# Decoder layer with 32 experts on one core: part of the first expert's weights loaded before the expert loop, routing and last layer norm in another order

## The reference, cut to what matters

```python
logits = xf @ w_router + b_router
top_logit, top_idx = lax.top_k(logits, 4)
gates = jax.nn.softmax(top_logit, axis=-1)
# for each expert e, on the rows that chose it
gu = xblk @ w_gate_up[e] + b_gate_up[e]          # 1024 -> 2048
g, u = jnp.split(gu, 2, axis=-1)
act = (jnp.clip(u, -7, 7) + 1.0) * jnp.minimum(g, 7) * jax.nn.sigmoid(1.702 * jnp.minimum(g, 7))
y_rows = act @ w_down[e] + b_down[e]             # 1024 -> 1024
# gated sum over the four experts of a row, then
x = layer_norm(ALPHA * x + y, ln3_g, ln3_b)
```

## Time and profile before

| what | value |
|---|---|
| median of three runs | 1255.53 us |
| profiled execution, its time | 1254.92 us |
| profiled execution, span of the profile | 1253.1 us |
| PE busy | 1193.6 us (95%) |
| DMA over the span | 485.46 MB, mean 387 GB/s |
| expert weights among it | 403 MB |
| granted TensorE clock, mean | 0.997 of full speed |

### The profile page before, as it was taken

One profiled execution on the slowest core, in us unless ns is written; L12 is line 12 of the kernel. 1 busy time (PEld: TensorE's weight loads), 2 busy tenths in 40 slices (PEclk: granted clock), 3 DMA queues, 4 the chain that ended last, 5 costly groups with the idle time before them and its releaser, 6 DMA issues.

```text
span 1253.1 us, 16715 instructions
## 1 busy us (share of the span) xinstructions
PE 1193.6 (95%) x6623; PEld 564.9 (45%) x6623; DVE 364.7 (29%) x909; ACT 233.5 (19%) x444; POOL 46.1 (4%) x84
## 2 busy tenths in 40 slices
PE   9999999999999999999989999898989899989997
PEld 8994477877343433434332333233333333333333
DVE  4747734635222130211212030302021221212132
ACT  4543312223220201102020201010110102020101
POOL 2201000101100000000000000000000000000001
PEclk9999999999999999999999999999999999999998
DMA  9995997989799999999999999999999999999994
GB/s 324 255 319 187 294 304 271 377 343 420 266 423 423 428 428 428 425 428 427 430 426 427 427 427 427 427 427 424 428 429 427 426 427 426 431 424 427 426 425 189
DMA packets 65349, 485.46 MB, mean 387 GB/s; under 512 B 6664, under 2 KB 7052, under 8 KB 37056
## 3 DMA queue, kind: packets, MB, share of 16 engines
q1 hardware_dynamic: 60896, 469.35, 92.6%
q0 software_dynamic: 4224, 15.48, 3.8%
q10 hardware_dynamic: 192, 0.11, 0.0%
HBM read 479.75 MB, written 5.17 MB: 387 GB/s over the span
## 4 chain that ended last, share of the span: by engine, by line
PE 63%; DMA 33%; DVE 2%; ACT 1%; SPq 1%; issue 1%; POOL 0%; DVEq 0%; POOLq 0%
PE ps L2255 27%; DMA late<-in_w_gate_up_dram 16%; DMA ring<-in_w_gate_up_dram 14%; PE ps L1781 11%; PE ps L2313 6%; PE ps L2295 5%; PE ps L1828 5%; DMA late<-in_w_down_dram 3%; PE ps L2219 1%; PE ps L1970 1%; PE ps L2321 1%; PE ps L1992 1%; PE ps L2141 1%; PE ps L2164 1%; PE ps L2280 0%
## 5 line engine op out<-in xcount | busy, mean ns | idle before, releaser
L2255 PE MATMUL ps<-ring,arena 128*64 128x512 f32 x1536 | 360.1, 600 | 13.5 <-DMA ring<-in_w_gate_up_dram 13.5
L1678 DVE TENSOR_TENSOR arena<-arena,ps 128x264 f32<-128x264 f32 x128 | 55.1, 431 | 576.3 <-PE ps L2313 576.3
L2255 PEld LDWEIGHTS ps<-ring,arena 128*64 128x64 f32 x1536 | 99.8, 136 | 198.6 <-issue 164.1
L2295 PE MATMUL ps<-ring,arena 128*64 128x512 f32 x768 | 171.9, 596 | 14.7 <-DMA ring<-in_w_down_dram 14.4
L1088 ACT ACTIVATE arena<-arena 128x512 f32<-128x512 f32 x32 | 20.2, 632 | 470.6 <-DVE arena L1661 470.6
L2295 PEld LDWEIGHTS ps<-ring,arena 128*64 128x64 f32 x768 | 53.8, 137 | 119.1 <-issue 105.2
L2313 PE MATMUL ps<-arena 128*128 128x264 f32 x256 | 91.3, 438 | 0.0
L2255 PE MATMUL ps<-late,arena 128*64 128x512 f32 x384 | 90.2, 598 | 0.0
L1781 PE MATMUL ps<-arena,ring 128*128 128x256 f32 x384 | 88.1, 380 | 0.0
L2313 PEld LDWEIGHTS ps<-arena 128*128 128x128 f32 x256 | 38.1, 188 | 103.8 <-issue 103.8
L1781 PEld LDWEIGHTS ps<-arena,ring 128*128 128x128 f32 x384 | 70.8, 189 | 10.9 <-issue 1.8
(11 more groups left out here) (329 smaller groups left out, 953.5 us busy)
## 6 DMA issues: line engine op xcount, KB each, us to landing
ring<-in_w_gate_up_dram SPq DMA_DIRECT2D x96, 2048.0 KB, 33.8
ring<-in_w_down_dram SPq DMA_DIRECT2D x40, 2048.0 KB, 34.4
late<-in_w_gate_up_dram SPq DMA_DIRECT2D x16, 2048.0 KB, 33.9
arena<-in_w_gate_up_dram SPq DMA_DIRECT2D x16, 1024.0 KB, 32.2
late<-in_w_gate_up_dram SPq DMA_DIRECT2D x16, 1024.0 KB, 34.1
late<-in_w_down_dram SPq DMA_DIRECT2D x8, 2048.0 KB, 35.3
ring<-in_w_in_dram SPq DMA_DIRECT2D x11, 1024.0 KB, 19.9
ring<-in_cache_mem_k_dram SPq DMA_DIRECT2D x8, 1024.0 KB, 6.5
```

Source lines behind the costliest of these rows:

```text
L1678: nc.vector.tensor_tensor(xT[:, c, :], xT[:, c, :], ps[:, 2 + c % 2, 0:T], ALU.add).then_inc(e_y_out, 1)
L2255: ins = mm(ps[64 * j:64 * j + 64, 6 * a + gu, :], x, w[:, D * gu + 512 * j:D * gu + 512 * j + 512], start=(c < 0), stop=(c == 7), skip_gro ...
L2295: ins = mm(ps[64 * j:64 * j + 64, 4 + half, :], x, w[:, kk, 512 * half:512 * half + 512], start=(m == 0), stop=(m == 7), skip_group_check= ...
```

## The change

1. SP gets two loads before the loop's own: 1 MB of `w_down` of expert 0 (its item 16, the first of unit 8) into `ahead`, which is the place of `xh2` and later `g3`, and 512 KB (half of item 17) into `ahead_third`, the place of `yo`. They wait for what POOL's gain loads waited for. The load of unit 8 is then 512 KB. The first `down` reads the three places.
2. POOL's 11 gain loads wait for `e_du` 1, the first down item read by PE, since `ahead` lies where `g3` goes.
3. DVE's `low_of(1)` comes after `select(0)`, and PE's `gather` takes the samples and tile 0 first and tile 1 after them, with a wait for `s_least` 2 between.
4. PE's first pair and second pair are written out before the loop, and the two register loads that the loop's bounds need come after them.
5. The tail takes the sample rows first on PE and DVE, and ACT issues three of the four sample stores, SP one.
6. Two single 128x128 products (`stay_awake`) are added on PE in the second layer norm.

```diff
+        ahead = view(m0 + 4864, 2, D)
+        ahead_third = view(a_tail, D)
...
+            sp.wait_ge(s_rt, 1)
+            sp.wait_ge(s_hi, 2)
+            sp.wait_ge(s_less, 2)
+            sp.dma_start(ahead.rearrange("p v n -> p (v n)"), first_down[:, 0, :]).then_inc(landed_part[0], 16)
+            sp.dma_start(ahead_third, first_down[:, 1, 0:D]).then_inc(landed_part[1], 16)
             for u in range(UNITS, ROUND // 2):
                 unit_read(0, u - UNITS)
-                unit_load(0, u)
+                if u == UNITS:
+                    sp.dma_start(expert_slot(2 * u + 1)[:, D:2 * D], first_down[:, 1, D:2 * D]).then_inc(
+                        unit_landed(u), 16)
+                else:
+                    unit_load(0, u)
...
-            pool.wait_ge(s_hi, 2)
-            pool.wait_ge(s_less, 2)
-            pool.wait_ge(s_rt, 1)
+            pool.wait_ge(e_du, 1)
             pool.dma_start(g3[:, 0, :], ln3_g.broadcast_to((P, D))).then_inc(s_g3, 16)
...
-                for b in range(2):
+                for b in range(3):
                     act.dma_start(y_sample.rearrange("b s d -> (b s) d")[:, 256 * b:256 * b + 256],
...
-            low_of(1)
             dve.wait_ge(s_rt_out, 1)
...
             select(0)
+            low_of(1)
...
+                if k == 1:
+                    stay_awake(1, ps[:, 5, 0:P])
                 pe.wait_ge(s_dn_out, 40 if k == 0 else 56)
...
+                    for t in range(2):
+                        for c in range(4 * half, 4 * half + 4):
...
+                            elif between and half == 0 and c == 0:
+                                pe.wait_ge(s_least, 2)
...
-            pairs = pe.value_load(nswi[0:1, 0:1], min_val=16, max_val=80)
-            last_round = pe.value_load(nswi[0:1, 2:3], min_val=7, max_val=39)
...
-            with pe.Fori(0, last_round) as r:
+            pair(0, 0, first=True)
+            pair(0, 1)
+            pairs = pe.value_load(nswi[0:1, 0:1], min_val=16, max_val=80)
+            last_round = pe.value_load(nswi[0:1, 2:3], min_val=7, max_val=39)
+            with pe.Fori(1, last_round) as r:
...
+            for half, h in ((0, 0), (1, 0), (0, 1), (1, 1)):
+                copied(half, h)
+                b = 2 * half + h
+                ins = mm(ps[32 * b:32 * b + 32, LASTB[2], 0:256], SelT[:, half, SROWS:SROWS + 32],
+                         yb[:, half, 256 * h:256 * h + 256], start=False, stop=True, skip_group_check=True)
+                if b == 0:
+                    last_scatter(LORDER[0], 0, 0)
             ins.then_inc(s_ln, 1)
```

More of the change, by code:

```diff
@@ L336, in decoder_layer @@
         g3s = view(a_bgu + D + D // 2, 2, 256)
+        ahead = view(m0 + 4864, 2, D)
+        ahead_third = view(a_tail, D)
         landed = [sem(f"landed{s}") for s in range(RING)]
         landed_extra = [sem(f"landed_extra{i}") for i in range(2)]
-        landed_end = [sem(f"landed_end{i}") for i in range(2)]
+        landed_part = [sem(f"landed_part{i}") for i in range(2)]
         s_const = sem("s_const")
@@ L732, in _ @@
             sp.wait_ge(s_yo, 2)
-            for b in range(2, 4):
-                sp.dma_start(y_sample.rearrange("b s d -> (b s) d")[:, 256 * b:256 * b + 256],
-                             yo[32 * b + 32 - NS:32 * b + 32, 2, 0:256]).then_inc(s_yst, 16)
+            sp.dma_start(y_sample.rearrange("b s d -> (b s) d")[:, 3 * 256:4 * 256],
+                         yo[P - NS:P, 2, 0:256]).then_inc(s_yst, 16)
             sp.wait_ge(s_yst, 16 * 6)
@@ L2069, in layer_norm @@
                         sample_rows()
+                if k == 1:
+                    stay_awake(1, ps[:, 1, 0:P])
                 for c in range(4, DC):
@@ L2281, in turn_act, with down @@
                 ins.then_inc(e_at, 1)
-            def down(r, k, behind=None):
+            def down(r, k, behind=None, first=False):
                 for i in range(4):
-                    item_arrived(pe, r, ITEM_AT[k, 8 + i])
                     w = expert_slot(ITEM_AT[k, 8 + i]).rearrange("p (k n) -> p k n", k=2)
+                    if first and i == 0:
+                        pe.wait_ge(landed_part[0], 16)
+                        w = ahead
+                    else:
+                        item_arrived(pe, r, ITEM_AT[k, 8 + i])
+                    w = [w[:, v, :] for v in range(2)]
+                    if first and i == 1:
+                        pe.wait_ge(landed_part[1], 16)
+                        w[0] = ahead_third
                     for kk in range(2):
@@ L2343, in samples_turned, with pair @@
                 mm(ps[:, LASTB[2], 256:512], ident, g3s[:, 1, :], start=False, stop=True, skip_group_check=True)
-            def pair(r, j, last=False):
+            def pair(r, j, last=False, first=False):
                 it = 2 * r + j
@@ L2356, in pair @@
                 pe.wait_ge(e_at_out, 2 * it + 2)
-                down(r, 2 * j, sum_first if last else None)
+                down(r, 2 * j, sum_first if last else None, first)
                 pe.wait_ge(e_act, 2 * it + 3)
```

81 lines of the change are left out of this document (42 added, 39 removed).

## The result

The changed kernel takes 1262.76 us (median of 5 runs, 1261.8 to 1264.75) where the kernel before takes 1255.53 (5 runs, 1254.86 to 1257.22): 1.0058 times, with a 95% interval of 1.0047 to 1.0068. That is slower, as forecast, but by 7.2 us and not by the forecast's 2.5 (1258.0 against 1255.53), and outside the range. The profiled execution after has 1262.76 us and a span of 1260.95, against 1254.92 and 1253.11: the spans differ by 7.8 us, and this is the number that the traces have to explain.

The account below looks back on a forecast made before the run. It took the continuous DMA weight stream at 427 GB/s, then 28 us of tail, as the bound. Terms -1.2 + 3.9 + 0 + 0 + 0.1 = +2.8 us on 1254.92 gave 1257.7, raised to 1258.0 toward the median; range 1254.6 to 1260.4.

Parts of the forecast that it names:

- 1.5 MB ahead: Weight loads from unit 8 on: loading 1.5 MB early shortens the stream, -1.2 us taken, bounds 0 to -2.2.
- gain loads in the plateau: POOL's gain loads, moved to about 359 us into the full DMA stream, cost +3.9 us.
- first expert's start: Selection, gather and loop entry on PE: first expert begins about 320.75 us, no change; bounds -0.5 to +0.7.
- tail: Kernel's end with sample rows first and stores split three to one: +0.1 us, bounds -0.5 to +0.6.
- between the unit that the row shows and the best case: Loads of units 9 to 13: -1.2 us, chosen between unit 9's 0.5 us gain and 2.2 us at best.
- 3.2 us of idle DMA: Between the rest of unit 8 and unit 9: 3.2 of the 3.7 us saved become a DMA gap.
- Both bounds, 3.2 and 4.55 us: Price of POOL's late gain loads: 3.2 us by bytes at 427 GB/s, 4.55 by engine time held; middle taken.
- rival that they run beside the stream: Late gain loads at 359 to 366 us: a second queue lifts the rate to some 600 GB/s, costing nothing; 12%.
- lower sum, -2.7: Whole kernel, gain loads free, loads ahead at their best, half of the start's 0.5 gained: -2.7 us, 1252.2.
- The register loads go behind the second pair: nothing: PE near 425 us: register loads placed there cost nothing, since PE runs ahead of the DMA.
- DVE starts about when it did: Tail: sample products, 0.64 us, precede the first tile's second scatter half, so DVE's start hardly moves.
- The first tile's scale comes some 0.5 us later: Tail on DVE: sample statistics come first, delaying the first tile's scale some 0.5 us, carried through POOL's passes to its store.

Follow-up runs that it names:

- not_ahead: The changed kernel with the 1 MB and 512 KB loads issued by SP in unit 8's old place instead of ahead: 1262.67 us, 1.0069.
- no_tail: The changed kernel with the old tail put back: 1262.46 us, 1.0056 times the kernel before.
- gains_late: The kernel before with only POOL's 11 gain loads made to wait for the first down item, nothing loaded ahead: 1259.74 us, 1.0034.
- selection_only: The kernel before with the remainder behind the selection, the new gather order and the two idle products: 1256.33 us, 1.0008.
- pairs_out: The kernel before with PE's first two pairs written out ahead of the loop and the register loads behind them: 1256.55 us, 1.0012.
- third_ahead: The changed kernel with the old tail, gain loads at their old time and only 512 KB loaded ahead: 1257.08 us, 1.0014.
- gains_by_sp: The kernel before with the gain loads late, issued by SP behind its unit 16 in the weights' queue: 1261.3 us, 1.0042.
- gains_twice_late: The kernel before with all gain loads late and done twice, one behind the other: 1265.57 us, 1.0077.

## Why the prediction was wrong

The bound was read rightly: a byte more in the plateau counts, PE follows the landings, and what is lost there stays to the end. The sign is right; three of the five terms are too good, and one is missing.

| step of the prediction | its value, us | the traces |
| --- | --- | --- |
| 1.5 MB ahead | -1.2 | 0 (not_ahead) |
| gain loads in the plateau | +3.9 (3.2 to 4.55) | +4.5 to 5.2 (weights missing while they run); 1.0034 and 1.0042 in time |
| first expert's start | 0 | -0.1 (320.72 against 320.80) |
| code of the written-out pairs | not in the sum | +1.3 |
| tail | +0.1 (-0.5 to +0.6) | +1.3 |

**The loads ahead.** The step "between the unit that the row shows and the best case" failed. It held that all above 7.5 us from issue to landing is queue, so that unit 9 would gain up to 0.5 us and units 10 to 13 more. With the 1.5 MB gone from before it unit 9 took 8.0 us (no_tail: 7.6), and 8.0 to 9.4 in the other fifteen traces, which don't have them ahead; so it may gain a little, more than one pair of executions can tell. But nothing of it lasts: in not_ahead the units behind it land no later. The 3.2 us of idle DMA that the text foresaw are there; they were all that is left of the effect.

**The gain loads.** The mechanism was right: POOL's packets now run in the plateau (362.9 to 388.5 us, where 359 and 4 us were said), and the landings are late by a constant from then on. The price was not. Both bounds, 3.2 and 4.55 us, price the gain packets alone, and for these the sum was good: they held 3.7 us of all engines. The step that failed is that it put at nothing what they do to the weight packets beside them. Those took 2.63 us per MB in place of 2.35 while the nine small loads ran, and with that the loads cost 4.5 us (gains_late) to 5.2 (not_ahead), read as the weights that are missing while POOL's packets run; the changed kernel has 5.1. By the rule quoted from the Trainium skill ("DMA: Bandwidth & Descriptors", Specifications), line rate from 512 B on, it would be 3.2 us. The two large loads, with rows of 4 KB, agree with it (2.6 us for 2.5 by bytes); the small ones, with rows of 512 B and 1 KB, don't (2.4 for 0.9). There measurement and rule differ, and the measurement decides. The rival that they run beside the stream fell: 403 GB/s in 370 to 380 us, not 600. (Its lower sum, -2.7, is also not what its parts give: -2.2, half of -0.5 and +0.1 make -2.35.)

**Selection, gather and loop entry.** Right, part by part: the gates come later and PE waits for them (+0.77 in selection_only, 0.7 said), the register loads' 0.85 us go (-0.91 in pairs_out, -0.75 said). "About 320.75" stands at 320.72.

**The written-out pairs.** "The register loads go behind the second pair: nothing" looked at the time of PE alone. The code itself was not priced. The row was on the page of the kernel before, the count of code packets; that one holds a DMA engine for about 1 us while the stream has no slack was not read from it.

**The tail.** Two steps failed. "DVE starts about when it did": it starts 0.7 us later, because the sample products that its first statistics wait for end only at 1246.8: two of the eight run at 1245.00, six behind a product of the first tile, at 1246.18. "The first tile's scale comes some 0.5 us later": 1.29. And the path was left open; the text took DVE for the chain, whose last pass ends 0.78 us later behind the copies, and its stores for the end. The end hangs on the pass that the same sentence named, POOL's, and takes over the 1.3 in full.

The times by parts (4.3 to 6.0 for the gain loads, 1.7 for third_ahead, 1.7 for the tail) sum to 7.7 to 9.4 with intervals of about 1 us either way; the changed kernel's 7.2 lies just below. The traces add up more closely: 5.2 + 1.3 + 1.3 = 7.8.

## What to carry to other kernels

Where each issue waits for a reader, moving bytes ahead of the stream shortens nothing; ask which issue comes earlier by it, and if none does, count zero. Work that ran in a quiet stretch must not be moved into a saturated one at the price of its bytes, nor at that of its own packets' engine time: ask as well what the packets of the stream cost while it runs (here 12% more beside loads of small rows, nothing beside rows of 4 KB). In a kernel whose DMA engines are full, code is traffic too: count the code packets of the page before a loop is written out. And before a tail is reordered, look for the engine whose last pass stands at one fixed distance from the span's end in every trace.

## What was not expected of the hardware

- In the full weight stream a packet of code of 16 KB holds one DMA engine for 1.02 to 1.11 us, and five more of them cost 1.3 us, nine more 2.8.
- The eleven gain loads, 576 packets and 1.38 MB, cost 4.5 to 5.2 us in that stream, in a queue of their own or in that of the weights, though POOL's packets held only 3.7. The two with rows of 4 KB cost their bytes (2.6 us for 1.04 MB); beside the nine small ones the weights took 2.63 us per MB in place of 2.35.
- With 1.5 MB less ahead of it, a 2 MB load still landed 8.0 us after its issue (7.6 in no_tail), and 330 to 340 us ran at 342 GB/s; the same bytes in place (not_ahead) gave 416.
- POOL's closing drain lasts 7.19 us, 5.2 of them behind a last pass that takes 2.0. It lasts 6.29 us where POOL issued eleven loads fewer (gains_by_sp) and 8.09 where it issued eleven more (gains_twice_late). The cause is open.
